# Convolution: which engine multiplies and sums the taps

## What is computed

```python
CONV_WIDTH = 31
def conformer_conv(h, w_pw1, b_pw1, w_dw, b_dw, ln_g, ln_b, w_pw2, b_pw2):
    u = h @ w_pw1 + b_pw1
    a, gate = jnp.split(u, 2, axis=-1)
    u = a * jax.nn.sigmoid(gate)
    u = lax.conv_general_dilated(
        u, w_dw[:, None, :].astype(u.dtype),
        window_strides=(1,), padding=[(CONV_WIDTH - 1, 0)],
        dimension_numbers=("NWC", "WIO", "NWC"),
        feature_group_count=D_MODEL) + b_dw
    u = jax.nn.silu(layernorm(u, ln_g, ln_b))
    return u @ w_pw2 + b_pw2
```

## Time and profile before

| | |
|---|---|
| median of 3 runs | 2295.85 us (2295.7 to 2296.21) |
| profiled execution | span 2293.8 us, 2.05 us under the median; no other time of it is given |
| PE busy | 2270.3 us, 99% |
| DVE busy | 1338.0 us, 58% |
| ACT busy | 880.9 us, 38% |
| POOL busy | 256.3 us, 11% |
| PE's granted clock | 9 or more tenths in all 40 slices |
| convolution's stage | tiles 2 to 7 from 836.6 to 985.3 us |

### The profile page before, as it was taken

The page is one execution under the profiler, slowest core; times in us unless marked ns, Lnnn a source line. Parts: engine busy times, 40 slices in busy tenths (PEclk is TensorE's granted clock), DMA queues, the critical chain, the costliest instruction groups (busy, mean ns, idle before and its releaser), DMA issues.

```text
span 2293.8 us, 32791 instructions
## 1 busy us (share of the span) xinstructions
PE 2270.3 (99%) x11064; PEld 1840.3 (80%) x11064; DVE 1338.0 (58%) x1913; ACT 880.9 (38%) x1372; POOL 256.3 (11%) x212
## 2 busy tenths in 40 slices
PE   8999999999999999999999999999999999999998
PEld 6777778888888888868888888887777888888887
DVE  5557756543434779965465445486665646454555
ACT  6675645442324521233332222244444333222222
POOL 2022101211010400004040000040000404000003
PEclk9999999999999999999999999999999999999999
...
DMA packets 395616, 202.79 MB, mean 88 GB/s; under 512 B 13792, under 2 KB 393200, under 8 KB 395520
## 3 DMA queue, kind: packets, MB, share of 16 engines
...
## 4 chain that ended last, share of the span: by engine, by line
PE 88%; issue 6%; DVE 2%; ACT 2%; POOL 1%; DMA 1%; DVEq 0%; SPq 0%; ACTq 0%; POOLq 0%
PE bank L1783 24%; PE bank L1785 23%; PE bank L1784 23%; PE bank L2168 2%; PE bank L2160 2%; PE bank L1763 2%; PE bank L2188 1%; PE bank L2266 1%; PE bank L2243 1%; PE bank L2339 1%; PE bank L2375 1%; PE bank L2077 1%; PE bank L2079 1%; PE bank L2078 1%; DVE m_w_lo L1121 1%
## 5 line engine op out<-in xcount | busy, mean ns | idle before, releaser
L608 ACT ACTIVATE m_w_hi<-m_raw 128x1024 fp32r<-128x1024 f32 x332 | 351.5, 1059 | 879.7 <-PE bank L1785 846.7
L1783 PE MATMUL bank<-m_h_hi,m_w_hi 128*128 128x512 f32 x1504 | 608.5, 405 | 2.2 <-DVE m_w_lo L1121 1.2
L1785 PE MATMUL bank<-m_h_hi,m_w_lo 128*128 128x512 f32 x1504 | 587.0, 390 | 0.0
L1784 PE MATMUL bank<-m_h_lo,m_w_hi 128*128 128x512 f32 x1504 | 586.4, 390 | 0.0
L1121 DVE TENSOR_TENSOR m_w_lo<-m_raw,m_w_hi 128x1024 fp32r<-128x1024 f32 x332 | 440.2, 1326 | 92.2 <-ACT m_w_hi L608 87.3
L1783 PEld LDWEIGHTS bank<-m_h_hi,m_w_hi 128*128 128x128 f32 x1504 | 282.8, 188 | 65.9 <-issue 4.7
L1785 PEld LDWEIGHTS bank<-m_h_hi,m_w_lo 128*128 128x128 f32 x1504 | 282.4, 188 | 60.4
L1784 PEld LDWEIGHTS bank<-m_h_lo,m_w_hi 128*128 128x128 f32 x1504 | 283.1, 188 | 55.5 <-issue 2.4
L1783 PE MATMUL bank<-m_f_hi,m_w_hi 128*128 128x512 f32 x688 | 268.7, 391 | 0.2 <-DVE m_w_lo L1121 0.2
L1785 PE MATMUL bank<-m_f_hi,m_w_lo 128*128 128x512 f32 x688 | 267.8, 389 | 0.0
L1784 PE MATMUL bank<-m_f_lo,m_w_hi 128*128 128x512 f32 x688 | 267.7, 389 | 0.0
...
## 6 DMA issues: line engine op xcount, KB each, us to landing
m_raw<-in_ff_w SPq DMA_DIRECT2D x256, 256.0 KB, 3.0
...
```

Source lines behind the costliest of these rows:

```text
L608: act.activation(WH[:, v % 2], RAW[:, v % 2], ACT.Copy).then_inc(s.w_hi, 1)
L1783: pe.matmul(o, high[:, r, k, :], hi, start=start, stop=False)
L1784: pe.matmul(o, high[:, r, k, :], lo, start=False, stop=False)
L1785: last = pe.matmul(o, low[:, r, k, :], hi, start=False, stop=stop)
```

## The change

- `PE_TAPS` is gone. DVE does 19 taps of a tile (DVE_TAPS = 31 - 12), cut at 8 and 14. The other 12 (SUM_TAPS) are multiplied by ACT, each into one of four product tiles `PROD` in SBUF, and summed by POOL with 11 additions into `SUMS[m % 2]`. ACT's product j waits for addition j - 4, which frees its product tile; POOL's addition j waits for product j.
- ACT's `conv_steps(m)` makes products 0 to 5 of tile m - 1 before its first split and 6 to 11 between the first and the second.
- `tile_done` waits for the taps and the additions, adds `SUMS` to the even sum, and the odd sum to that, in SBUF. The line numbers move: L1492 becomes L1520, L1488 L1516, L1497 L1527, L1509 L1543, L1121 L1149, L608 L622, L2188 L2217.
- The last tile has 9 taps on PE (in the bank `GB[0]`), 8 on ACT and POOL (SUM_TAPS_LAST, 7 additions), 14 on DVE, and a third addition at its end for PE's bank.
- Five semaphores of the first block's lambda become one that counts to five; the instructions there are the same.

```diff
@@ -21,9 +21,10 @@
 FOX_HEADS = 16
 MEM_HEADS = 4
 TAPS = 31
-PE_TAPS = 3
+SUM_TAPS = 12
+SUM_TAPS_LAST = 8
 PAD = TAPS - 1
-PE_TAPS_LAST = 14
+PE_TAPS_LAST = 9
 EPS = 1e-6
 LN_EPS = 1e-5
 NEG = -1e30
...
@@ -210,6 +211,8 @@
         CA = at("conv_a", 186, [P, T])
         CG = at("conv_g", 188, [P, T])
         LZ = at("conv_odd", 182, [P, T])
+        PROD = [at(f"tap_product{i}", 120 + 2 * i, [P, T]) for i in range(4)]
+        SUMS = [at(f"tap_sum{i}", kb, [P, T]) for i, kb in enumerate((184, 194))]
         LG = at("ln_sq", 194, [P, T])
         LY = at("ln_y", 196, [P, T])
         WHM = at("w_hi_more", 24, [P, 2, KD, P], F32R)
...
@@ -585,6 +588,17 @@
                 pool.tensor_tensor(MX[:, k, :], MX[:, k, :], RSM[:], ALU.mult).then_inc(s.mem_normed, 1)
             x_squares()
 
+            for m in range(KD):
+                total = SUMS[m % 2][:]
+                for j in range(1, SUM_TAPS if m < KD - 1 else SUM_TAPS_LAST):
+                    if j == 1 and m >= 2:
+                        pool.wait_ge(s.cv_tile, m - 1)
+                    if j > 1:
+                        pool.drain()
+                    pool.wait_ge(s.cv_prod, m * SUM_TAPS + j + 1)
+                    pool.tensor_tensor(total, PROD[0][:] if j == 1 else total, PROD[j % 4][:], ALU.add)\
+                        .then_inc(s.cv_added, 1)
+
             for layer in range(2):
                 x_squares()
                 x_squares()
...
@@ -912,17 +926,30 @@
                 o = MV[layer][:, :, m * P:(m + 1) * P] if isinstance(m, int) else MV[layer][:, :, bass.ds(m * P, P)]
                 act.activation(o, bank[:, 0:MEM].rearrange("p (a b) -> p a b", b=P), ACT.Copy).then_inc(s.mem_out, 1)
 
+            def products(m, first, last, n=SUM_TAPS, beside=0):
+
+                at_start = isinstance(m, int) and m == 0
+                if first == 0:
+                    act.wait_ge(s.cv_u, m + 1)
+                for j in range(first, last):
+                    if j >= 4:
+                        act.wait_ge(s.cv_added, m * (SUM_TAPS - 1) + max(j - 4, 1))
+                    elif not at_start:
+                        act.wait_ge(s.cv_added, (m - 1) * (SUM_TAPS - 1) + SUM_TAPS - 4 + j)
+                    k = TAPS - beside - n + j
+                    act.activation(PROD[j % 4][:], UP[:, k:k + T], ACT.Identity,
+                                   scale=span(VEC[:], m + (TAP_COL + KD * k), 1)).then_inc(s.cv_prod, 1)
+
             def conv_steps(m):
                 first = isinstance(m, int) and m == 0
                 q = 0 if first else m * 3 + 3
                 if first:
                     norm()
                 else:
-                    for j in range(PE_TAPS):
-                        c = TAP_COL + KD * (TAPS - PE_TAPS + j)
-                        act.activation(DIAG[:, j, :], IDENT, ACT.Identity, scale=span(VEC[:], m + (c - 1), 1))\
-                            .then_inc(s.cv_diag, 1)
+                    products(m - 1, 0, SUM_TAPS // 2)
                 step(None)
+                if not first:
+                    products(m - 1, SUM_TAPS // 2, SUM_TAPS)
                 step(None)
                 if not first:
                     mem_key(0, m, q, SBK[1])
...
@@ -937,17 +964,18 @@
                     for j in range(3):
                         mem_value(1, j, 3 + j, SBK[1 + j])
 
-            def last_diagonals(first, last, done):
-                for j in range(first, last):
+            def last_diagonals():
+                for j in range(PE_TAPS_LAST):
                     c = TAP_COL + KD * (TAPS - PE_TAPS_LAST + j) + KD - 1
-                    act.activation(DIAG[:, j, :], IDENT, ACT.Identity, scale=VEC[:, c:c + 1]).then_inc(done, 1)
+                    act.activation(DIAG[:, j, :], IDENT, ACT.Identity, scale=VEC[:, c:c + 1])\
+                        .then_inc(s.cv_diag, 1)
 
             conv_steps(0)
-            last_diagonals(PE_TAPS, PE_TAPS_LAST, s.cv_diag_last)
+            last_diagonals()
             conv_steps(1)
             with U.loop(act, KD - 2, 2) as i:
                 conv_steps(i + 2)
-            last_diagonals(0, PE_TAPS, s.cv_diag)
+            products(KD - 1, 0, SUM_TAPS_LAST, SUM_TAPS_LAST, PE_TAPS_LAST)
             for j in range(3):
                 mem_value(1, 3 + j, 27 + j, SBK[1 + j])
             for k in range(KD):
...
@@ -1470,7 +1498,7 @@
 
 
             dve.memset(UP[:, 0:PAD], 0.0)
-            DVE_TAPS = TAPS - PE_TAPS
+            DVE_TAPS = TAPS - SUM_TAPS
 
             def column(c):
                 return VEC[:, c:c + 1]
...
@@ -1493,15 +1521,21 @@
                     tap.then_inc(s.cv_tap, 1)
 
             def tile_done(m, n):
+                x = CV[:, m, :]
                 dve.wait_ge(s.cv_tap, DVE_TAPS * m + n)
-                dve.tensor_tensor(LY[:], LY[:], LZ[:], ALU.add)
+                dve.wait_ge(s.cv_added, m * (SUM_TAPS - 1) + (SUM_TAPS if m < KD - 1 else SUM_TAPS_LAST) - 1)
+                dve.tensor_tensor(x, LY[:], SUMS[m % 2][:], ALU.add)
                 dve.drain()
-                dve.wait_ge(s.cv_pe, m + 1)
-                dve.tensor_tensor(pick(CV, m), LY[:], SBK[0][:], ALU.add).then_inc(s.cv_tile, 1)
+                last = dve.tensor_tensor(x, LZ[:], x, ALU.add)
+                if m == KD - 1:
+                    dve.drain()
+                    dve.wait_ge(s.cv_pe, 1)
+                    last = dve.tensor_tensor(x, GB[0][:], x, ALU.add)
+                last.then_inc(s.cv_tile, 1)
                 dve.drain()
 
             def conv_steps(m, prev):
-                cut = [0, 12, 20, DVE_TAPS]
+                cut = [0, 8, 14, DVE_TAPS]
 
                 def gated():
                     up = UP[:, PAD:PAD + T]
...
@@ -1531,8 +1565,8 @@
             conv_steps(1, 0)
             for m in range(2, KD):
                 conv_steps(m, m - 1)
-            taps(KD - 1, 0, TAPS - PE_TAPS_LAST)
-            tile_done(KD - 1, TAPS - PE_TAPS_LAST)
+            taps(KD - 1, 0, TAPS - PE_TAPS_LAST - SUM_TAPS_LAST)
+            tile_done(KD - 1, TAPS - PE_TAPS_LAST - SUM_TAPS_LAST)
             dve.wait_ge(s.ln_mean, 1)
             for k in range(KD):
                 dve.tensor_tensor(CV[:, k, :], CV[:, k, :], TR[:], ALU.subtract).then_inc(s.ln_c, 1)
...
@@ -2175,20 +2209,13 @@
                 first, last = isinstance(m, int) and m == 0, isinstance(m, int) and m == KD - 1
                 return pe.matmul(TR[:], MEAN, pick(CV, m), start=first, stop=last)
 
-            def taps_of(m, first, last, n=PE_TAPS):
-
-                def f():
-                    if first == 0:
-                        pe.wait_ge(s.cv_u, m + 1)
-                        pe.wait_ge(s.cv_diag, m * PE_TAPS + PE_TAPS)
-                        if n > PE_TAPS:
-                            pe.wait_ge(s.cv_diag_last, n - PE_TAPS)
-                    for j in range(first, last):
-                        k = TAPS - n + j
-                        mm = pe.matmul(SBK[0][:], DIAG[:, j, :], UP[:, k:k + T], start=(j == 0), stop=(j == n - 1))
-                    if last == n:
-                        mm.then_inc(s.cv_pe, 1)
-                return f
+            def last_taps():
+                pe.wait_ge(s.cv_u, KD)
+                pe.wait_ge(s.cv_diag, PE_TAPS_LAST)
+                for j in range(PE_TAPS_LAST):
+                    k = TAPS - PE_TAPS_LAST + j
+                    mm = pe.matmul(GB[0][:], DIAG[:, j, :], UP[:, k:k + T], start=(j == 0), stop=(j == PE_TAPS_LAST - 1))
+                mm.then_inc(s.cv_pe, 1)
 
             def conv_units(m, prev=None, before=None):
                 if prev is None:
...
@@ -2200,8 +2227,6 @@
                 if prev is None:
                     pe.wait_ge(s.mn, 2 * KD)
                 mem_key(0, 0, m, q, SBK[1])
-                if prev is not None:
-                    taps_of(prev, 0, PE_TAPS)()
                 mem_value(0, 1, m, q + 1, SBK[2])
                 if before is not None:
                     conv_mean(before)
...
@@ -2218,7 +2243,7 @@
             mem_value(1, 3, 1, 27, SBK[1])
             mem_value(1, 0, KD, 28, SBK[2])
             conv_mean(KD - 2)
-            taps_of(KD - 1, 0, PE_TAPS_LAST, PE_TAPS_LAST)()
+            last_taps()
             mem_value(1, 1, KD, 29, SBK[3])
             conv_mean(KD - 1).then_inc(s.ln_mean, 1)
             for k in range(KD):
```

More of the change, by code:

```diff
@@ L1191, in lambda_dots @@
                     dve.reduce_sum(SMALL[0:1, 10 + i:11 + i], LAMS[0:1, 2 * i, :], AX.X)
-                dve.drain().then_inc(s.lam_dots, 1)
+                dve.drain().then_inc(s.lam, 1)
             def kept(k):
@@ L1847, in lambda_to_all @@
             def lambda_to_all():
-                pe.wait_ge(s.lam_one, 1)
-                pe.matmul(OB[:, 0:1], ONES[0:1, :], SMALL[0:1, 15:16], start=True, stop=True).then_inc(s.lam_all, 1)
+                pe.wait_ge(s.lam, 3)
+                pe.matmul(OB[:, 0:1], ONES[0:1, :], SMALL[0:1, 15:16], start=True, stop=True).then_inc(s.lam, 1)
             def plain(ready=None):
```

(1 more changed line is left out.)

13 lines of the change are left out of this document (6 added, 7 removed).

## The result

| | before | changed |
|---|---|---|
| time, median | 2295.89 us (2295.7 to 2296.21, 4 runs) | 2324.72 us (2324.35 to 2324.92, 4 runs) |
| span of the profiled execution | 2293.8 us | 2323.1 us |
| one steady tile of the convolution | 24.78 us | 29.11 us |

The changed kernel is slower: ratio 1.0125, 95% interval 1.0111 to 1.0139. The forecast was 2323 us, 1.7 us under it, and the range of 2308 to 2342 holds it.

What follows compares the result with a forecast made beforehand. PE and DVE were both full in the convolution, PE deciding; the change would make DVE the bound. +26.5 + 5.8 - 6.2 + 1.0 = +27.1 us on the 2293.8 us span gave a 2323 us median, range 2308 to 2342.

Steps and rivals of the forecast that it cites:

- PE's need for a tile: Steady convolution tiles: without its three taps of 0.86 us each, PE needs 22.20 us a tile instead of 24.78.
- DVE's own work: Steady convolution tiles: with nine taps fewer and a 0.34 us wait gone, DVE needs 18.4 us, before delays by POOL.
- The price of a sum: Steady tiles: each POOL addition delays a two-SBUF-input DVE instruction by 1.04 us; 10.7 us a tile, cycle 29.2 us.
- the walk: Steady tile followed from L1488: eleven sums among DVE's instructions, the sixth hiding 0.69 us beside the bank's scaling, last over at 20.3.
- The price of break-even: Steady tiles: the delay per POOL sum at which the change neither gains nor loses, (24.78 - 18.4) / 11 = 0.58 us.
- rival 3: Convolution: the delay is the whole 1.29 us instruction, or ACT's queue is late too; cycle 31.9 us, 2344 us, chance 0.13.
- First tile: Convolution's first tile: five fewer taps -3.3 us, DVE's later low half +1.4, sums in the way +7.8; together +5.8 us.
- Last tile: Convolution's last tile, L1488 to the first subtraction: 19.5 us instead of 25.7, so 6.2 us less.
- Slow matmuls after PE's pause: Layer norm's sums, after PE stands for 7 us before the last mean: 1.0 us added, bounds 0 to 2.5.
- The sum: Whole kernel: +26.5 steady tiles, +5.8 first tile, -6.2 last tile, +1.0 slow matmuls, together +27.1 us.
- The signs named ahead: Changed profile: L1516 every 29 us, taps alternating 0.75 and 1.78 us, group mean about 1.3, PE waiting some 7 us a tile.
- ACT's products: Convolution: twelve products of 0.63 us each, 7.6 us a tile, bringing ACT to some 11.6 us, far below the bound.

Runs made afterwards that it cites:

- sums in PSUM: Changed kernel with DVE's even and odd running sums in two PSUM banks instead of SBUF: 2274.4 us, ratio 0.9908 against the kernel before.
- one column: Changed kernel with ten of POOL's eleven additions a tile on one column instead of 512, waits and products kept: 2275.54 us.
- write only: Changed kernel with every POOL addition in the convolution replaced by a memset of the same tile, which reads nothing: 2274.53 us.
- filling the pause: Changed kernel with seven unread float32 matmuls in PE's pause before the last tile's mean: 2322.37 us, ratio 1.0117 against the kernel before.
- the dummy taps: Changed kernel with three unread float32 matmuls of the taps' size put back on PE in each of the first seven tiles: 2324.29 us.
- products of one column: Changed kernel with ACT's products on one column instead of 512, except the stage's first four; POOL's additions whole: 2324.91 us.

## Why the prediction was right, step by step

**PE's need for a tile** was put at 22.20 us. Where the taps were undisturbed, the cycle was 22.32 (sums in PSUM), 22.11 (one column) and 22.03 us (write only). Right within 0.2 us.

**DVE's own work** was 18.4 us. The ten long taps cost 1.01 to 1.04 us over 0.74, and the split at 881.13 cost 0.47 over 1.22: some 10.6 us. 29.11 - 10.6 = 18.5 us, by subtraction.

**The price of a sum** was the deciding term, 1.04 us from one collision in a quite other stage. It measured 1.02 in most taps (1.76 against 0.74), with eleven sums a tile, one of them hidden in part beside the bank's scaling at 880.53 as in the walk. The sum was 10.7 and is 10.6; the cycle was 29.2 and is 29.11. A reader should notice what carried this: the row was of the same shapes and the same number of SBUF inputs, and the old convolution had no row for it at all. The price of break-even, 0.58 us, lay far enough below 1.04 for the sign to be safe.

**The whole-instruction rule** (rival 3) would have been 1.29 us. The page of the Trainium skill named in the prediction (SBUF — State Buffer, Who interferes with whom; the whole instruction stands for this pair in its section SBUF: two separate sides) is right on who meets whom, and the runs show it from both sides: one SBUF input on DVE, or no reading on POOL, and the delay is gone. On the size the measurement decides: a tap loses 1.02 us of POOL's 1.29, in a pair that repeats every 1.68 us (875.18 to 876.86 in POOL's timeline).

**First tile**: forecast +5.8 us, measured 842.56 - 836.60 = +6.0. DVE's low half starts at 821.83, 1.46 us later than before, against 1.4 in the forecast:

```profile
821.83 1.64 DVE L1149 TENSOR_TENSOR m_w_lo<-m_raw,m_w_hi 128x1024 fp32r<-128x1024 f32 x1 [1.81 <-ACT m_w_hi L622]
```

**Last tile**: forecast -6.2 us. It measured 20.4 us from L1516 (1017.20) to L1572 (1037.62), -5.3. DVE's part was right: 1017.20 to the end of L1533 at 1035.45 is 18.25 us, against 18.5. The 0.9 us are the mean matmul, 2.08 us where I had 1.0, less the quarter of a microsecond that DVE was early.

**Slow matmuls after PE's pause** is the term that was mis-sized: 1.0 us, bounds 0 to 2.5. I had put it in for the layer norm's sums alone, and these cost 13.83 - 11.94 = 1.9 us, inside the bounds; the mean matmul ahead of them was put at its fast 1.0 us and costs 1.1 us more. Together the slow matmuls cost 3.0 us. I had read the effect of a pause off as one slow matmul, and that reading was wrong. In the kernel before, this is the row of PE's timeline ahead of them:

```profile
7.60 3.65 PE L1763 MATMUL bank<-m_con,m_x_rows 128*128 128x128 f32 x16 [7.60 <-DMA m_x_rows<-in_x]
```

The pause of 7.6 us ends here. The matmul of 0.79 us at 11.70 came 4.1 us later, behind sixteen others, so the row shows how long after a pause a matmul was still slow and not that only one is. In the changed kernel too, between 1036 and 1045 us the clock is at 0.50 and then 0.68, and through that stretch DVE, ACT and PE wait for each other in turn, so that each slow matmul stands on the path. What filling the pause did (above) shows it as cause: 2.8 of the 3.0 us came back.

**The sum.** Measured parts: 6 x (29.11 - 24.78) = +26.0, first tile +6.0, last tile -5.3, behind it +1.9; together +28.6 of the span's +29.3. The forecast's +27.1 was 26.5 + 5.8 - 6.2 + 1.0. At the first L1583 the two traces are 28.5 us apart (1051.45 and 1022.96), so the remaining 0.7 us arise in later stages; what makes them isn't shown. That the forecast came within 1.7 us is luck in part: the steady tiles were 0.5 us too dear and both ends together 2.0 too cheap, and the median lies 1.6 us over the span here, not the 2.05 that I had carried over.

**The signs named ahead.** L1516 every 29 us; the taps at 0.75 and 1.76 us; a group mean of 1.291 us and POOL's sums at 1.575, one every 1.68:

```profile
L599 POOL TENSOR_TENSOR m_tap_sum<-m_tap_sum,m_tap_product 128x512 f32<-128x512 f32 x76 | 119.7, 1575 | 12.1 <-issue 11.9
L1520 DVE SCALAR_TENSOR_TENSOR m_ln_y<-m_padded,m_vec,m_ln_y 128x512 f32<-128x512 f32 x69 | 89.1, 1291 | 0.0
```

The last sum was to be over six microseconds ahead of L1527 and is, by 5.9. One sign was off: PE was to wait some 7 us a tile and be at 97%, and it waits 25.66 / 6 = 4.3 us and is at 98%. The missing part is in its granted clock: 0.91 over the stage, so that PE is busy for 148.98 us with matmuls for which it needs 133.88 at 1.00 (the kernel with sums in PSUM). That cost nothing, since DVE was late anyway; the dummy taps raised the clock to 0.97 and the time stayed.

**ACT's products** were taken at 0.63 us from a square and take 0.72. With twelve a tile it is 1.1 us on an engine that is idle for more than half of the stage, and the run with products of one column shows that even all of it is worth nothing.

What stays open: why a tap loses 1.02 us and not POOL's whole 1.29. The runs show that the delay grows with the columns that POOL reads (0.47 us for 256, 1.02 for 512), and that an addition of one column still lasts 0.41 us (in the run of that name), so that a part of each addition doesn't go with its data. Which part holds DVE up, no run shows.
